# A two-layer fp32 trunk: activations and residual blocks turned through VectorE and device memory instead of TensorE

## The chip, the cores and the metric

One core of one Trainium2 chip runs the whole program in one launch. The metric is the device time of that launch in microseconds (us), median of several runs. Everything is computed and stored in fp32.

## What is computed

A sequence of 256 tokens with 2048 channels goes through two layers. Layer one is a Mamba-2 mixer, layer two a differential attention; a squared-ReLU MLP with 8192 hidden channels follows each of the two. Cut to what matters here:

```
h = h + mamba2_mixer(rms_norm(h, ssm_norm_w), ...)        # ends in y @ w_out, (256, 4096) @ (4096, 2048)
h = h + sq_relu_mlp(rms_norm(h, mlp_norm_w[0]), w_up[0], w_down[0])
k, v = shared_kv(h, kv_norm_w, w_kv, k_norm_w)
h = h + diff_attention(rms_norm(h, attn_norm_w), k, v, w_q, ..., w_o)
h = h + sq_relu_mlp(rms_norm(h, mlp_norm_w[1]), w_up[1], w_down[1])

def sq_relu_mlp(h, w_up, w_down):                          # w_up (2048, 8192), w_down (8192, 2048)
    return jnp.square(jax.nn.relu(h @ w_up)) @ w_down
```

## The kernel before

**Pieces.** All weights pass through the core once, in 865 pieces of 128 x 1024 numbers (512 KB). SyncE loads a piece into one of four slots of `w_raw`. ScalarE rounds it to the matmul's reduced fp32 format (`hi`, L739), VectorE subtracts the rounded part from the original (`lo`, L1093), and TensorE multiplies three times: stationary hi by weight hi (L366), hi by lo (L367), lo by hi (L368). In the stages around the change a piece is two tiles of 128 input channels by 512 output columns, so it costs 2 tiles x 2 token halves x 3 = 12 matmuls of 512 columns (`piece`, L351 to L369). The slots form a ring of four: `hi` of piece j waits until TensorE has finished piece j - 4 (semaphore `w_used`), and a load waits for `lo_made` of the piece four before.

**Order of work.** Every engine walks through the same list of pieces. All its other steps are written at hand-chosen places of this list: "if j == 2" means after the engine's own step for piece j. An engine does its steps in order, so a step that waits holds up the later pieces' `hi` or `lo`.

**MLP.** A chunk is 64 pieces. Its first 32 make four blocks u = 0..3 of 512 hidden channels (8 pieces each, `up`), its last 32 add the chunk's share to the four output blocks d = 0..3 (`down`). Each MLP has four chunks. A finished block u is read by ScalarE (`relu`, L919) and VectorE (`square`, L1298) into the buffer `act`, which has tokens on the partitions. The next product needs it with channels on the partitions, as the stationary operand `st`. So TensorE turns it: `turn_up` (L567) is eight 128 x 128 transposes through the identity matrix (L374) into a PSUM bank pair `aux`, and ScalarE (`up_hi`, L923) and VectorE (`up_lo`, L1302) split it from there into hi and lo.

**Residual blocks.** `h` is kept with tokens on the partitions. When a block n of 512 columns has been updated (`add_resid`, L1258 to L1268), `turn_resid` (L511) turns it on TensorE in the same way, and ScalarE (L744) and VectorE (L1098) split it with the norm's weight, once for the next MLP, twice for the attention (one copy for keys and values, one for queries).

**Banks.** Products alternate between the two PSUM bank pairs `acc[0]` and `acc[1]`; `aux[0]` and `aux[1]` hold turned blocks and the attention's or the scan's intermediate results.

**GpSimd.** Its instructions of the mixer end before the first MLP; after that it makes two masks and, once for every norm, a reciprocal square root (L1487).

The places of the steps, in pieces after the piece that completes a block, are these: add or relu and square two or three steps later, turn on TensorE after the third piece, split at the sixth. One table sets an order of pieces by hand:

```
WO_ORDER = ([(n, k) for n in (0, 1) for k in range(0, 12, 2)] + [(n, k) for n in (0, 1) for k in (12, 14)]
            + [(n, k) for n in (2, 3) for k in range(0, KT, 2)])
```

It is the list of (output block, input channel tile) for 32 pieces. The tiles 12 to 15 of block 0 come only after tiles 0 to 11 of block 1, so that the last quarter of the stationary operand is needed twelve pieces after the start and not six. Before the change only the attention's output product uses it.

## Time and profile before

| what | value |
|---|---|
| median of 3 runs | 2549.56 us (2549.36 to 2550.37) |
| the profiled execution | 2549.55 us, of which the trace spans 2547.9 us |
| TensorE matmul busy | 2524.6 us, 99% of the span |
| VectorE busy | 1477.1 us, 58% |
| ScalarE busy | 1194.0 us, 47% |
| GpSimd busy | 210.2 us, 8% |
| mean granted TensorE clock | 0.999 |

The span is the time from the first to the last instruction of the trace. The rest of the execution, 1.65 us, lies around it. Matmul durations in the rows overlap, since a matmul is drained while the next one streams; the pace is the distance between two starts.

### The profile page before, as it was taken

How to read it: one execution, taken by the hardware profiler on the slowest of the kernel's cores; microseconds unless marked ns; L12 is line 12 of the kernel's file. 1: busy time of each engine (PE TensorE's matmuls, PEld its weight loads, DVE VectorE, ACT ScalarE, POOL GpSimd, SP SyncE). 2: the span in 40 equal slices, each digit the busy share in tenths (PEclk: the TensorE clock that was granted, in tenths of full speed). 3: DMA queues.
4: the chain of work that ended last, by engine and by line, in shares of the span. 5: the costliest groups of instructions: out<-in, count | busy, mean ns of one | idle time of the engine just before them, and what ended most of it. 6: DMA issues, size and time to landing. Idle time of an engine off the chain costs nothing.

```text
span 2547.9 us, 33913 instructions
## 1 busy us (share of the span) xinstructions
PE 2524.6 (99%) x12081; PEld 2117.9 (83%) x12081; DVE 1477.1 (58%) x1508; ACT 1194.0 (47%) x1460; POOL 210.2 (8%) x115
## 2 busy tenths in 40 slices
PE   8999999999999999999999999999999999999999
PEld 7888888888888888888888888888888888888887
DVE  5777777775555555555555655666555555555554
ACT  5455555554444344344344545555544444443443
POOL 2433233330000000000000000000000000000000
PEclk9999999999999999999999999999999999999999
DMA  7555555554566565666665565554565666666664
GB/s 220 171 181 181 176 178 171 175 180 167 182 198 182 193 191 184 193 187 190 191 187 182 178 203 167 164 176 162 174 194 188 189 189 190 190 184 195 190 187 167
DMA packets 266592, 468.14 MB, mean 184 GB/s; under 512 B 17198, under 2 KB 50320, under 8 KB 265472
## 3 DMA queue, kind: packets, MB, share of 16 engines
q1 hardware_dynamic: 264736, 457.87, 58.6%
q0 software_dynamic: 1472, 8.79, 1.0%
q8 instruction: 72, 1.18, 0.2%
q14 instruction: 24, 0.20, 0.0%
q10 hardware_dynamic: 288, 0.11, 0.0%
HBM read 464.54 MB, written 2.16 MB: 183 GB/s over the span
## 4 chain that ended last, share of the span: by engine, by line
PE 88%; DVE 4%; issue 2%; POOL 2%; DMA 2%; ACT 2%; DVEq 0%; SPq 0%; ACTq 0%; POOLq 0%
PE acc L366 25%; PE acc L368 25%; PE acc L367 25%; PE aux L366 2%; PE aux L374 2%; PE aux L367 2%; PE aux L368 2%; DVE w_lo L1093 2%; DMA work<-decay_rows 1%; POOL work L1543 1%; POOL work L1541 1%; DVE work L1180 1%; ACT w_hi L739 1%; PE aux L435 1%; PE aux L434 1%
## 5 line engine op out<-in xcount | busy, mean ns | idle before, releaser
L1093 DVE TENSOR_TENSOR w_lo<-w_raw,w_hi 128x1024 fp32r<-128x1024 f32 x865 | 1121.4, 1301 | 821.4 <-ACT w_hi L739 819.9
L739 ACT ACTIVATE w_hi<-w_raw 128x1024 fp32r<-128x1024 f32 x865 | 913.3, 1060 | 1007.5 <-PE acc L368 904.6
L366 PE MATMUL acc<-w_hi,stationary 128*128 128x512 f32 x3200 | 1256.5, 393 | 1.9 <-DVE w_lo L1093 0.7
L368 PE MATMUL acc<-w_hi,stationary 128*128 128x512 f32 x3200 | 1246.4, 389 | 0.0
L367 PE MATMUL acc<-w_lo,stationary 128*128 128x512 f32 x3200 | 1245.7, 389 | 0.0
L368 PEld LDWEIGHTS acc<-w_hi,stationary 128*128 128x128 f32 x3200 | 600.6, 188 | 125.8
L366 PEld LDWEIGHTS acc<-w_hi,stationary 128*128 128x128 f32 x3200 | 601.0, 188 | 124.5 <-issue 1.1
L367 PEld LDWEIGHTS acc<-w_lo,stationary 128*128 128x128 f32 x3200 | 601.2, 188 | 121.2
L1487 POOL TENSOR_TENSOR small<-small 128x2 f32<-128x2 f32 (+2 forms) x22 | 38.3, 1744 | 1207.2 <-DVE small L1103 1207.2
L366 PE MATMUL aux<-w_hi,stationary 128*128 128x256 f32 (+1 forms) x384 | 123.8, 322 | 3.4 <-DVE w_lo L1093 3.4
L368 PE MATMUL aux<-w_hi,stationary 128*128 128x256 f32 (+1 forms) x384 | 122.2, 318 | 0.0
L367 PE MATMUL aux<-w_lo,stationary 128*128 128x256 f32 (+1 forms) x384 | 122.2, 318 | 0.0
L1302 DVE TENSOR_TENSOR stationary<-aux,stationary 128x1024 fp32r<-128x1024 f32 x32 | 39.2, 1224 | 74.5 <-ACT stationary L923 74.5
L366 PEld LDWEIGHTS aux<-w_hi,stationary 128*128 128x128 f32 x384 | 73.1, 190 | 10.9 <-DVE w_lo L1093 6.0
L374 PE MATMUL aux<-ident,work 128*128 128x128 f32 x576 | 75.7, 273 | 2.9 <-ACT work L824 2.9
L374 PEld LDWEIGHTS aux<-ident,work 128*128 128x128 f32 x576 | 66.7, 141 | 14.3 <-ACT work L824 5.9
L368 PEld LDWEIGHTS aux<-w_hi,stationary 128*128 128x128 f32 x384 | 73.0, 190 | 5.0
L367 PEld LDWEIGHTS aux<-w_lo,stationary 128*128 128x128 f32 x384 | 73.1, 190 | 4.9
L923 ACT ACTIVATE stationary<-aux 128x1024 fp32r<-128x1024 f32 x32 | 32.9, 1027 | 80.9 <-PE aux L374 80.9
L1098 DVE SCALAR_TENSOR_TENSOR stationary<-aux,params,stationary 128x256 fp32r<-128x256 f32 (+1 forms) x104 | 42.7, 474 | 44.3 <-ACT stationary L744 44.3
L1298 DVE SCALAR_TENSOR_TENSOR work<-acc,work 128x1024 f32<-128x1024 f32 x32 | 39.2, 1224 | 47.1 <-ACT work L919 47.1
L1555 POOL TENSOR_TENSOR work<-work 128x1024 f32<-128x1024 f32 (+1 forms) x16 | 59.7, 3729 | 59.1 <-ACT work L795 37.0
(173 smaller groups left out, 929.4 us busy)
## 6 DMA issues: line engine op xcount, KB each, us to landing
w_raw<-in_w_up SPq DMA_DIRECT2D x256, 512.0 KB
w_raw<-in_w_down SPq DMA_DIRECT2D x256, 512.0 KB
w_raw<-in_ssm_w_in SPq DMA_DIRECT2D x129, 512.0 KB
w_raw<-in_ssm_w_out SPq DMA_DIRECT2D x64, 512.0 KB
w_raw<-in_w_kv SPq DMA_DIRECT2D x64, 512.0 KB
w_raw<-in_ssm_w_in SPq DMA_DIRECT2D x64, 256.0 KB
w_raw<-in_w_q SPq DMA_DIRECT2D x32, 512.0 KB
w_raw<-in_w_o SPq DMA_DIRECT2D x32, 512.0 KB
```

The costliest lines, as they stand in the source:

```text
L366: pe.matmul(o, xh, hi[:, k], start=start, stop=False)
L367: pe.matmul(o, xh, lo[:, k], start=False, stop=False)
L368: mm = pe.matmul(o, xl, hi[:, k], start=False, stop=stop)
L374: tr = pe.transpose(dst(i, t), src(i, t), ident[:, :])
L739: a.activation(whi[:, s, :], raw[:, s, :], ACT.Copy).then_inc(sem("hi_made"), 1)
L923: a.activation(st[:, RB + 4 * u:RB + 4 * u + 4, 0, :], whole(aux[u % 2]), ACT.Copy).then_inc(sem("turned_hi"), 1)
L1093: v.tensor_tensor(wlo[:, s, :], raw[:, s, :], whi[:, s, :].bitcast(F32), ALU.subtract).then_inc(sem("lo_made"), 1)
L1098: ins = v.scalar_tensor_tensor(one_tile(st, kt + i, 1), turned_tile(bank, i), param(w + i), one_tile(st, kt + i, 0).bitcast(F32), ALU.mult ...
L1298: v.scalar_tensor_tensor(act, acc[u % 2][:, :, :], 0.0, act, ALU.max, ALU.mult).then_inc(sem("up_read"), 1)
L1302: v.tensor_tensor(st[:, RB + 4 * u:RB + 4 * u + 4, 1, :], whole(aux[u % 2]), st[:, RB + 4 * u:RB + 4 * u + 4, 0, :].bitcast(F32), ALU.subt ...
L1487: gp.tensor_tensor(out, in_, nhalf[:, 0:out.shape[1]], ALU.pow).then_inc(sem(signal), 1)
L1555: gp.tensor_tensor(m, m, c.unsqueeze(1).to_broadcast([P, HG, c.shape[1]]), ALU.mult).then_inc(sem("m_made"), 1)
```

## The change

The eight transposes of a block on TensorE go. In their place:

1. `turn` on VectorE: one instruction transposes each 32 x 32 square of the 128 x 1024 block, from `act` or `h` into the buffer `squares_t`.
2. `spread(n)` on GpSimd's queue: one DMA writes `squares_t` to a 512 KB scratch tensor in device memory; after it has landed, four DMAs, each for 32 partitions, read the squares back into `channels` in the places that they have in a full transpose. GpSimd does this 44 times. Both buffers lie in the arena `work`, in the place of the attention's `kT` and `qT`.
3. `resid_hi`, `resid_lo`, `up_hi`, `up_lo` read `channels` instead of `aux`.
4. The MLPs use all four bank pairs, block u or d in `banks[u]`, and their down products and first up products follow `WO_ORDER`. So does the first key and value product of the attention. SyncE loads the pieces in the same order.
5. The places of the steps are now in three tables, each row (block, piece that completes it, piece after which it is read and turned, piece after which it is split).

The diff, cut:

```
+UPS = ((0, 7, 10, 16), (1, 15, 18, 24), (2, 23, 26, 32), (3, 31, 34, 40))
+UPS_FIRST = ((0, 13, 15, 22), (1, 15, 17, 27), (2, 23, 26, 32), (3, 31, 34, 40))
+DOWNS = ((0, 45, 47, 54), (1, 47, 49, 59), (2, 55, 58, None))
+PLAIN = [(n, k) for n in range(4) for k in range(0, KT, 2)]
...
+        squares_t, channels = kT.rearrange("p s t -> p (s t)"), qT.rearrange("p s t -> p (s t)")
+        spread_dram = nc.dram_tensor("spread", [TT, 4, 32, 4, P], F32).ap()
+        banks = acc + aux
...
         def _(pe):
-            def turn_resid(n, added, turned):
-
-                pe.wait_ge(sem("resid_added"), added)
-                transposes(to_channels(aux[n % 2]), lambda i, t: h[:, t, n * NB + i * P:n * NB + (i + 1) * P]).then_inc(sem("turned"), 1)
...
+                def up(c, fresh):
+                    for i, (u, kt) in enumerate(WO_ORDER if fresh else PLAIN):
+                        if kt == 0:
+                            pe.wait_ge(sem("resid_added"), R + 4 * c + u - 3 if c else R - 1 if u == 0 else R)
+                        if fresh and u == 0 and kt % 4 == 0:
+                            pe.wait_ge(sem("turned_lo"), T - 3 + kt // 4)
+                        piece(Pos(base, c, PER_CHUNK), i, banks[u], NB, RA + kt, kt == 0, kt == KT - 2)
+
+                def down(c):
+                    for i, (d, kt) in enumerate(WO_ORDER):
+                        if kt == 0:
+                            pe.wait_ge(sem("up_read"), c * 4 + (U + d + 1))
+                        if d == 0 and kt % 4 == 0:
+                            pe.wait_ge(sem("turned_lo"), c * 4 + (T + 1 + kt // 4))
+                        piece(Pos(base, c, PER_CHUNK), 32 + i, banks[d], NB, RB + kt, kt == 0, kt == KT - 2)
...
         def _(act_e):
             def resid_hi(n, turned, targets):
-                a.wait_ge(sem("turned"), turned)
+                a.wait_ge(sem("spread"), turned * 64)
...
                 def up_hi(c, u):
+                    a.wait_ge(sem("spread"), c * 256 + (T + u + 1) * 64)
+                    a.activation(st[:, RB + 4 * u:RB + 4 * u + 4, 0, :].rearrange("p k (b i) -> p k b i", i=32),
+                                 channel_tiles, ACT.Copy).then_inc(sem("turned_hi"), 1)
...
         def _(v):
+            def turn(src, n):
+
+                wait(v, sem("spread_out"), (n - 1) * 16)
+                v.transpose(squares_t.rearrange("p (t q k i) -> p t k q i", q=4, k=4, t=TT),
+                            src.rearrange("p t (k q i) -> p t k q i", k=4, q=4)).then_inc(sem("turned"), 1)
...
                 def square(c, u):
 
                     v.wait_ge(sem("relu_made"), c * 4 + (U + u + 1))
-                    v.scalar_tensor_tensor(act, acc[u % 2][:, :, :], 0.0, act, ALU.max, ALU.mult).then_inc(sem("up_read"), 1)
+                    v.scalar_tensor_tensor(act, banks[u][:, :, :], 0.0, act, ALU.max, ALU.mult).then_inc(sem("up_read"), 1)
+                    v.wait_ge(sem("up_read"), c * 4 + (U + u + 1))
+                    turn(act, c * 4 + (T + u + 1))
...
+                        for d, last, at_add, at_lo in DOWNS:
+                            if j == at_add:
+                                add_resid(d, Pos(base, c, PER_CHUNK), last, True, banks[d])
+                                if carry:
+                                    turn_resid(d, R + 13 + d, T_carry + d + 1)
+                            if j == at_lo and carry:
+                                resid_lo(d, T_carry + d + 1, after)
...
         def _(gp):
+            def spread(n):
+
+                gp.wait_ge(sem("turned"), n)
+                wait(gp, sem("spread"), (n - 1) * 64)
+                gp.dma_start(spread_dram.rearrange("t b c q f -> (b c) t (q f)"),
+                             squares_t.rearrange("p (t f) -> p t f", t=TT)).then_inc(sem("spread_out"), 16)
+                gp.wait_ge(sem("spread_out"), n * 16)
+                wait(gp, sem("turned_lo"), n - 1)
+                for q in range(4):
+                    gp.dma_start(channels[32 * q:32 * q + 32, :].rearrange("c (b f) -> c b f", f=P),
+                                 spread_dram[:, :, :, q, :].rearrange("t b c f -> c (t b) f")).then_inc(sem("spread"), 16)
```

`carry` is true in the last chunk of the first MLP, whose updated residual blocks go to the attention. The attention's output product uses the rows of `DOWNS` less 32. A last block (n = 3) is always added and turned after the third piece of the next stage and split after its ninth.

How instructions move, at three places. On TensorE in the first MLP, where block u = 1 of the first chunk is turned, the order before is (matmul rows L366 to L368 are the three products, L374 the transposes, `lo_made`, `turned_lo`, `up_read`, `resid_added` semaphores):

```order
L368 MATMUL acc<-w_hi,stationary 128x512
L374 MATMUL aux<-ident,work 128x128 [waits turned_lo,up_read]
L374 MATMUL aux<-ident,work 128x128 x7
L366 MATMUL acc<-w_hi,stationary 128x512 [waits lo_made]
L367 MATMUL acc<-w_lo,stationary 128x512
```

Now, in the same stretch of the program, block u = 2 begins in a bank pair `aux` and nothing stands between the pieces:

```order
L396 MATMUL acc<-w_hi,stationary 128x512
L394 MATMUL aux<-w_hi,stationary 128x512 [waits lo_made,resid_added]
L395 MATMUL aux<-w_lo,stationary 128x512
L396 MATMUL aux<-w_hi,stationary 128x512
L394 MATMUL aux<-w_hi,stationary 128x512
```

Over the whole program, TensorE's list has 61 groups of L374 before and 17 of the same line (now L402) after: 44 groups have gone. On VectorE, after block u = 0 of the first chunk (`w_lo` is the piece's `lo`, `work` the activation buffer), before:

```order
L1298 SCALAR_TENSOR_TENSOR work<-acc,work 128x1024 [waits relu_made]
L1091 REGISTER_ALU
L1093 TENSOR_TENSOR w_lo<-w_raw,w_hi 128x1024 [waits hi_made]
L1091 REGISTER_ALU
L1093 TENSOR_TENSOR w_lo<-w_raw,w_hi 128x1024 [waits hi_made]
L1091 REGISTER_ALU
L1093 TENSOR_TENSOR w_lo<-w_raw,w_hi 128x1024 [waits hi_made]
L1301 REGISTER_ALU
L1302 TENSOR_TENSOR stationary<-aux,stationary 128x4x256 [waits turned_hi]
```

and now, with the transpose of squares after each square, two blocks read two pieces apart, and the split moved away:

```order
L1284 SCALAR_TENSOR_TENSOR work<-acc,work 128x1024 [waits relu_made]
L1244 STREAM_TRANSPOSE work<-work 128x2x4x4x32 [waits spread_out,up_read]
L1063 TENSOR_TENSOR w_lo<-w_raw,w_hi 128x1024 [waits hi_made] x2
L1284 SCALAR_TENSOR_TENSOR work<-acc,work 128x1024 [waits relu_made]
L1244 STREAM_TRANSPOSE work<-work 128x2x4x4x32 [waits spread_out,up_read]
L1063 TENSOR_TENSOR w_lo<-w_raw,w_hi 128x1024 [waits hi_made] x5
L1291 TENSOR_TENSOR stationary<-work,stationary 128x4x256 [waits turned_hi]
```

On GpSimd, right behind the masks, where nothing stood before but the norm's root, 44 groups like these two now follow, split by the attention's roots:

```order
L1557 DMA spread<-work 128x2x512 [waits spread,turned]
L1562 DMA work<-spread 32x8x128 [waits turned_lo,spread_out]
L1562 DMA work<-spread 32x8x128 x3
L1557 DMA spread<-work 128x2x512 [waits spread,turned]
L1562 DMA work<-spread 32x8x128 [waits turned_lo,spread_out]
```

The reads wait twice: for their own write to land, and until VectorE has split the block before (`turned_lo`), since there is one `channels` buffer.

## Rows read from the trace of the kernel before

**Rows 1.** The page: busy time, share of the span and instructions of each engine

```profile
PE 2524.6 (99%) x12081; PEld 2117.9 (83%) x12081; DVE 1477.1 (58%) x1508; ACT 1194.0 (47%) x1460; POOL 210.2 (8%) x115
```

**Rows 2.** Windows: chunk-long stretches of both MLPs, each engine's busy us, clock, DMA, GB/s

```profile
core 0: us, PE busy (x) PEld busy (x) DVE busy (x) ACT busy (x) POOL busy (x), PEclk, DMA share, GB/s
760.00:938.00 178.00, 178.00 (x803) 147.76 (x802) 93.05 (x81) 75.22 (x72) 0.00 (x0) 1.00 0.63 190
2014.00:2192.00 178.00, 178.00 (x803) 147.73 (x803) 92.72 (x80) 75.56 (x73) 0.00 (x0) 1.00 0.63 189
```

**Rows 3.** Waits of TensorE: who it waited for, us in total, times, longest

```profile
PE aux L366 <- DVE w_lo L1093: 3.4, 6, 0.6
PE acc L366 <- DVE stationary L1098: 0.6, 1, 0.6
```

**Rows 4.** Timeline of TensorE: two turns one chunk apart, then one turn with its neighbours

```profile
760.87 1.04 PE L374 MATMUL aux<-ident,work 128*128 128x128 f32 x8
...
938.55 1.04 PE L374 MATMUL aux<-ident,work 128*128 128x128 f32 x8
...
1316.11 0.39 PE L367 MATMUL acc<-w_lo,stationary 128*128 128x512 f32 x1
1316.33 0.40 PE L368 MATMUL acc<-w_hi,stationary 128*128 128x512 f32 x1
1316.57 1.04 PE L374 MATMUL aux<-ident,work 128*128 128x128 f32 x8
1317.36 0.48 PE L366 MATMUL acc<-w_hi,stationary 128*128 128x512 f32 x1
1317.68 0.40 PE L367 MATMUL acc<-w_lo,stationary 128*128 128x512 f32 x1
```

**Rows 5.** Timelines after a block ends: TensorE's next matmul, ScalarE, VectorE

```profile
1308.40 0.39 PE L366 MATMUL acc<-w_hi,stationary 128*128 128x512 f32 x1
...
1308.60 1.03 ACT L919 ACTIVATE work<-acc 128x1024 f32<-128x1024 f32 x1 [1.60 <-PE acc L368]
...
1309.66 1.22 DVE L1298 SCALAR_TENSOR_TENSOR work<-acc,work 128x1024 f32<-128x1024 f32 x1 [1.40 <-ACT work L919]
1310.80 1.21 DVE L1093 TENSOR_TENSOR w_lo<-w_raw,w_hi 128x1024 fp32r<-128x1024 f32 x1
```

**Rows 6.** Groups of instructions by form: VectorE's and ScalarE's passes

```profile
L1302 DVE TENSOR_TENSOR stationary<-aux,stationary 128x1024 fp32r<-128x1024 f32 x32 | 39.2, 1224 | 74.5 <-ACT stationary L923 74.5
L923 ACT ACTIVATE stationary<-aux 128x1024 fp32r<-128x1024 f32 x32 | 32.9, 1027 | 80.9 <-PE aux L374 80.9
L889 ACT ACTIVATE work<-resid 128x512 f32<-128x512 f32 x24 | 14.9, 623 | 1.7 <-DVE resid L1267 0.6
```

**Rows 7.** Timelines of ScalarE and VectorE: a residual block split twice; an add

```profile
1453.58 3.03 ACT L744 ACTIVATE stationary<-aux,params 128x256 fp32r<-128x256 f32 x8 [2.48 <-PE aux L374]
...
1456.64 3.23 DVE L1098 SCALAR_TENSOR_TENSOR stationary<-aux,params,stationary 128x256 fp32r<-128x256 f32 x8 [4.28 <-ACT stationary L744]
...
2522.14 1.41 DVE L1267 SCALAR_TENSOR_TENSOR resid<-acc,small,resid 128x512 f32<-128x512 f32 x2 [0.34 <-PE acc L368]
```

**Rows 8.** DMA issues: KB each, median us from issue to landing

```profile
work<-decay_rows POOLq DMA_DIRECT2D x8, 1024.0 KB, 5.0
resid<-in_x SPq DMA_DIRECT2D x4, 512.0 KB, 7.5
out<-resid SPq DMA_DIRECT2D x3, 512.0 KB, 5.9
out<-resid SPq DMA_DIRECT2D x2, 256.0 KB, 2.2
decay_rows<-work POOLq DMA_DIRECT2D x1, 64.0 KB, 2.0
```

**Rows 9.** The page, DMA queues: packets, MB, share of 16 engines; a GpSimd issue

```profile
q1 hardware_dynamic: 264736, 457.87, 58.6%
...
L1528 POOL DMA_DIRECT2D work<-decay_rows x8 | 4.9, 612 | 215.3 <-PE aux L435 213.7 <-DMA decay_rows<-work 1.7
```

**Rows 10.** Waits of ScalarE for weight loads, the two longest totals

```profile
ACT w_hi L739 <- DMA w_raw<-in_ssm_w_in: 14.1, 10, 2.0
ACT w_hi L739 <- DMA w_raw<-in_w_down: 9.4, 4, 3.0
```

**Rows 11.** Timeline of VectorE in the mixer, a `lo` beside a GpSimd pass

```profile
122.37 3.01 DVE L1093 TENSOR_TENSOR w_lo<-w_raw,w_hi 128x1024 fp32r<-128x1024 f32 x1 [2.35 <-ACT w_hi L739]
```

More of the change, by code:

```diff
@@ L957, in _ @@
+                chunk(0, True, False)
+                with a.Fori(1, 3) as c:
+                    chunk(c, False, False)
+                chunk(3, False, after is not None)
             mlp(UP0, R_MLP0, T_MLP0, 0, T_MLP0_END, to_mlp0, to_att)
@@ L1347, in _ @@
+                chunk(0, True, False)
+                with v.Fori(1, 3) as c:
+                    chunk(c, False, False)
+                chunk(3, False, after is not None)
             mlp(UP0, R_MLP0, T_MLP0, 0, T_MLP0_END, to_mlp0, to_att,
```

287 lines of the change are left out of this document (118 added, 169 removed).

## The prediction

> **What bounds the kernel now.** I read the page first: TensorE's matmuls are busy for 99% of the span, VectorE for 58%, ScalarE for 47% [rows 1]. Such a share could still hide pauses inside a stage, so the windows come next: a stretch of 178 us in either MLP shows matmuls for all of it, at full clock, with VectorE busy half of the time and the DMA engines 63% [rows 2]. Then the waits: what TensorE waited for is a few us in all, a total of 3.4 us being the largest one on the path of the pieces [rows 3]. So every us of TensorE's own work that goes shortens the run, and every us by which another engine makes it wait lengthens it. VectorE and ScalarE need only keep ahead.
>
> **What goes: 44 turns.** The order lists show 44 groups of eight transposes fewer on TensorE: 12 residual blocks and 2 x 16 activation blocks. The price of one is read from starts, since durations overlap. The last matmul before a turn starts at 1316.33, the second after it at 1317.68 [rows 4]: 1.35 us where two pitches would stand. The pitch comes from two turns one chunk apart: 938.55 - 760.87 = 177.68 us hold 64 x 12 matmuls and four turns [rows 4]. With c = 1.35 - 2p, 768p + 4c = 177.68 gives p = 0.2267 us and c = 0.897 us. The rows are rounded to 10 ns, so I take 0.895: 44 x 0.895 = **39.4 us** off the bound engine. A piece is 12p = 2.72 us.
>
> **What comes: nothing on TensorE, but three chains that must stay hidden.** Let t be the moment at which TensorE starts the piece after the one that completes a block.
>
> *First chain, the ring.* TensorE may run on while VectorE reads and turns the block. Before, relu starts 0.20 after t and square follows; the next `lo` starts 2.40 after t and ends at 3.61 [rows 5]. Now the transpose of squares stands between, of length T. It waits for the square's own semaphore, say 0.1, so the next `lo` ends at about 3.7 + T. In most places three pieces are ready by then (8.16 us), so T may be 4.4. Tight are the blocks u = 0 and 1 of each MLP's first chunk, read two pieces after they end: two pieces ready, 5.44 us, T up to 1.7. The same distance holds for d = 0 and 1 where residual blocks are turned (end of MLP 0, attention's output product), but there the add costs 1.41 [rows 7] instead of relu and square: 0.2 + 1.41 + 0.1 + T + 1.21 leaves T up to 2.5. No transpose of squares is in this trace. The nearest rows are VectorE's passes over the same 128 x 1024 fp32: 1.22 [rows 6]; the dearest such pass, slowed beside GpSimd's work, is 3.01 [rows 11]. I take 1.22, since one operand streams through just as in the cheap ones and GpSimd now only issues DMAs. Cost 0. At 3.01 the four tight reads lose 1.3 each and the four tight adds 0.5 each: 7.2 us. That is the upper bound; below zero it can't be, as no wait of TensorE stood there.
>
> The Trainium skill (VectorE: DVE Perf Modes, The three transpose paths) gives 311 ns for one 128 x 128 bf16 transpose of squares; if a block costs eight of these, an estimate by this page of the Trainium skill, T is 2.5 us and the run loses 4 x 0.8 = 3.2 us more than in my sum. No row here has the operation. The same page's rules for kernel authors say to turn 128 x 128 on TensorE when PSUM is a fit destination, which speaks against this change; the trace shows why it need not hold here, as TensorE is the one engine without idle time [rows 1].
>
> *Second chain, the way through memory.* Square and transpose end at about 2.5 + T = 3.8 after t. Then GpSimd issues the write (0.61 an issue [rows 9]), waits until it lands, issues four reads, waits for the last. Landing times from issue are 2.0 us for 64 KB out, 5.9 for 512 KB out, 2.2 for 256 KB, 5.0 for 1 MB in beside the weight stream, 7.5 for 512 KB in at the very start [rows 8]. I take 5.0 for the write and for the last read, because this row is from the same queue under the same load: 3.8 + 5.0 + 3 x 0.61 + 5.0 + 0.2 = **15.8 us** after t; bounds 2.0 and 2.0 give 9.8, and 5.9 and 7.5 give 19.2. When is it needed? The split stands nine pieces after the block's last piece. TensorE wants the next `lo` at 9 x 2.72 = 24.5; before it come the hi split 1.03 and lo split 1.22 [rows 6] and that `lo`, 1.21, with hand-overs 3.7. So the landing may be as late as 20.8. ScalarE gets there at about 14.9 and waits a us, which costs nothing. Even the upper bound fits. The operand itself is needed later still, at the thirteenth down piece. Cost 0 for 32 activation blocks.
>
> *Third chain, residual blocks for the attention.* These are split twice, 3.03 on ScalarE and 3.23 on VectorE [rows 7], so the limit falls to 24.5 - 7.7 = 16.8 after t, against 2.9 + 5.0 + 1.8 + 5.0 + 0.2 = 14.9. In addition the reads of one block wait until the block before is split. Block 1 is the tight one: ScalarE squares block 2 first (two passes with their sums, 1.6 us [rows 6, 7]), is free 3.2 after the end of piece 55, and 7.7 later the next `lo` is done, at 10.9, where TensorE wants it at 4 x 2.72 = 10.9. Block 2 lands about 1.5 after ScalarE could take it and ends 0.4 before its limit. With the landing bounds instead, blocks 0 and 2 lose 1 to 2 us each and block 1 as much again: 0 to 5. I take **1.0** for the whole stage change. For MLP 1 the blocks are split once, which halves the splits, and it fits.
>
> *DMA.* A turn adds 0.5 MB out and 0.5 MB back, 46 MB in all. At the price of the weight queue, 58.6% of the span for 457.87 MB [rows 9], that is 5.9% more, so the share goes from 0.60 to 0.66. One turn's traffic can delay one weight load by about 3.3 us. ScalarE has waited for loads before, 3.0 us at most, and TensorE noticed none of it [rows 10], for three pieces are ready ahead. Cost 0, covered by the ring.
>
> *Bank pairs and the new orders* remove waits that already cost nothing [rows 3]. VectorE gets 44 x 1.22 = 54 us more, of the 1070 us in which it is idle. GpSimd's roots stand in line behind the spreads, and the attention's first use is now at its piece 16, so they are early. The tail after the last piece is the same.
>
> **Sum.** 2549.55 (the profiled execution; the median of the three runs is 2549.56, so no correction) - 39.4 + 1.0 = **2511.2 us**, 1.5% faster.
>
> **Rivals.**
> 1. *The issue of small row pieces makes GpSimd's queue slow, and the run is slower.* A turn has 256 rows of 2 KB out and 1024 of 512 B back, in five issues; the issue of 0.61 us [rows 9] was for fewer and longer rows. Each issue lies in the second chain: with 2.4 us each, four times the row, the landing moves from 15.8 to 15.8 + 5 x 1.8 = 24.8, TensorE waits 4.0 for each of 44 blocks, 2511 + 176 = 2687. It decides from 20.8 on; gain and loss meet at 20.8 + 0.9 = 21.7. For it: the shape is in no row. Against: one issue for 64 KB and one for 1 MB land with the difference of their bytes only [rows 8], and the upper bounds above leave 1.6 us of room. The Trainium skill (DMA: Bandwidth & Descriptors, Anatomy of one DMA) puts the generation of descriptors down as small, with many for little more, and a DMA at 2.0 us plus its bytes over 436 GB/s, which would make the landing 3.8 + 3.2 + 1.8 + 2.3 + 0.2 = 11.3; it also warns of a long delay when device memory is written. Chance 0.07.
> 2. *The transpose of squares takes several passes.* With T = 4 x 1.22 = 4.9: the 28 ordinary reads lose 0.5 each, the four tight ones 3.2, the four tight adds 2.4: 36 us, 2547, no change. For it: an fp32 element is four bytes and the pattern has five levels. Against: every fp32 pass in the trace goes at one pace. Chance 0.05.
> 3. *Weight loads come late.* If the mixed traffic holds up loads so that TensorE loses 0.5 us in each turn, 2511 + 22 = 2533. Against it is the reserve above. Chance 0.05.
>
> Remains 0.83 for the forecast. Its own range is from 2510 (no stall) to 2511 + 7 + 4 = 2522 (both upper bounds). **Range** 2509.5 to 2523: it leaves out all three rivals, 0.17, and little else. About 0.2% (5 us) is what a measurement of this kernel can tell from no change. Faster by more: forecast, rival 3 and a mild form of 2, 0.90; the same 0.03; slower 0.07.
>
> **What would show it.** In the profile after: matmul pitch 0.2267 and 174.1 us per chunk instead of 177.7; 352 transposes on TensorE fewer; a transpose row of about 1.2 us x44; ScalarE waiting about 1 us for the reads before each `up_hi`, and the last read landing near 16 us after t; a wait of TensorE for `lo` of 0 to 2 us at the start of the attention and nowhere else. Wrong would be: TensorE waiting for `lo` in every chunk (second chain or loads), or in the first chunks only (T over 1.7).

## The result: 25.1 us faster, 13 us less than forecast

| | before | after |
|---|---|---|
| median | 2549.55 us (2549.36 to 2550.37, 4 runs) | 2524.43 us (2523.01 to 2525.01, 4 runs) |
| ratio, 95% interval | | 0.990 (0.9883 to 0.9917) |
| the profiled execution, its span | 2549.55, 2547.9 | 2525.01, 2523.4 |
| mean granted TensorE clock | 0.999 | 0.998 |

The direction was right, the size was not: 2511.2 was forecast, and the measured median lies 1.4 us above the upper end of the range, 2523.0. In what follows t is, as in the prediction, the moment at which TensorE starts the piece after the one that completes a block.

The page after, busy time [rows 1], DMA queues [rows 9] and the two new kinds of issue on GpSimd's queue (median us from issue to landing in the last column of the last two rows):

```profile
PE 2490.2 (99%) x11729; PEld 2083.6 (83%) x11729; DVE 1523.5 (60%) x1552; ACT 1192.5 (47%) x1460; POOL 344.4 (14%) x335
...
q1 hardware_dynamic: 264736, 457.87, 59.0%
q0 software_dynamic: 16256, 54.94, 8.2%
...
L1557 POOL DMA_DIRECT2D spread<-work x44 | 31.9, 725 | 1226.0 <-DVE work L1244 1070.2
L1562 POOL DMA_DIRECT2D work<-spread x176 | 102.2, 587 | 168.5 <-DMA spread<-work 147.7
...
spread<-work POOLq DMA_DIRECT2D x44, 512.0 KB, 3.8
work<-spread POOLq DMA_DIRECT2D x176, 128.0 KB, 6.0
```

TensorE has the 352 transposes fewer. GpSimd's issues cost 0.725 us for the write and 0.587 for a read. The 6.0 us are the median of all 176 reads; the last of the four, for which ScalarE waits, lands a median of 7.4 us after its own issue in this trace. The same stretch of MLP 0 as in [rows 2]:

```profile
core 0: us, PE busy (x) PEld busy (x) DVE busy (x) ACT busy (x) POOL busy (x), PEclk, DMA share, GB/s
760.00:938.00 178.00, 178.00 (x787) 147.34 (x786) 100.61 (x88) 77.48 (x75) 15.22 (x25) 1.00 0.74 219
1390.00:1460.00 70.00, 60.19 (x255) 48.33 (x253) 41.08 (x60) 38.20 (x63) 10.71 (x16) 0.96 0.67 206
```

In the chunk TensorE is busy all the time at full clock, as hoped. The second row is the passage from MLP 0 to the attention, and there 70 us hold only 60.2 of matmuls, at a granted clock of 0.96. The waits name it. TensorE's rows for `lo` (L1063, which answers to L1093 in [rows 3]), then ScalarE's for DMAs, of which the weight loads answer to [rows 10]:

```profile
PE aux L394 <- DVE w_lo L1063: 8.8, 9, 2.2
PE acc L394 <- DVE w_lo L1063: 5.8, 2, 5.0
```

```profile
ACT stationary L895 <- DMA work<-spread: 84.1, 30, 6.4
ACT w_hi L712 <- DMA w_raw<-in_w_down: 19.8, 7, 6.4
ACT stationary L870 <- DMA work<-spread: 18.6, 8, 7.0
ACT w_hi L712 <- DMA w_raw<-in_w_up: 17.1, 11, 3.8
ACT w_hi L712 <- DMA w_raw<-in_w_kv: 7.1, 3, 4.2
```

**Where the time went.** Between 1398 and 1461 us TensorE stops four times. From start to start (a pitch is 0.227) the distances are 2.48 at 1398.32, 2.59 at 1414.30, 1.42 at 1432.03 and 5.44 at 1455.12; less the pitches 11.0 us, and 0.7 more in the first step after each. Behind the second and the fourth the matmuls start 0.427 apart for 7 and 10 steps, which is the lower of the clock's two levels, 1.2 GHz, and costs 17 x 0.2 = 3.4. Together 15.1 us. The forecast without any stall is 2549.55 - 39.4 = 2510.15, and the profiled execution took 14.9 more. So the budget closes: **39.4 us were gained as computed, and some 15 were given back in one place.** The fourth stop:

```profile
1455.12 0.39 PE L396 MATMUL acc<-w_hi,stationary 128*128 128x512 f32 x1
1460.56 0.79 PE L394 MATMUL acc<-w_hi,stationary 128*128 128x512 f32 x1 [5.05 <-DVE w_lo L1063]
1461.15 0.63 PE L395 MATMUL acc<-w_lo,stationary 128*128 128x512 f32 x1
```

How this comes about is read from three timelines of the same stretch (in brackets: idle time before the row and what ended it). ScalarE:

```profile
1392.06 1.06 ACT L712 ACTIVATE w_hi<-w_raw 128x1024 fp32r<-128x1024 f32 x1 [4.48 <-DMA w_raw<-in_w_down]
1393.03 3.29 ACT L870 ACTIVATE stationary<-work,params 128x256 fp32r<-128x256 f32 x8
...
1406.50 1.06 ACT L712 ACTIVATE w_hi<-w_raw 128x1024 fp32r<-128x1024 f32 x1 [6.36 <-DMA w_raw<-in_w_down]
...
1409.10 3.31 ACT L870 ACTIVATE stationary<-work,params 128x256 fp32r<-128x256 f32 x8 [1.54 <-DMA work<-spread]
...
1425.66 3.31 ACT L870 ACTIVATE stationary<-work,params 128x256 fp32r<-128x256 f32 x8 [3.00 <-DMA work<-spread]
...
1452.78 3.31 ACT L870 ACTIVATE stationary<-work,params 128x256 fp32r<-128x256 f32 x8 [6.99 <-DMA work<-spread]
```

VectorE, from the split of block 0 (L1257) to the add of block 3 (L1238) and the split of block 3:

```profile
1396.35 3.26 DVE L1257 SCALAR_TENSOR_TENSOR stationary<-work,params,stationary 128x256 fp32r<-128x256 f32 x8 [1.97 <-ACT stationary L870]
1399.52 4.62 DVE L1063 TENSOR_TENSOR w_lo<-w_raw,w_hi 128x1024 fp32r<-128x1024 f32 x4
...
1429.00 3.26 DVE L1257 SCALAR_TENSOR_TENSOR stationary<-work,params,stationary 128x256 fp32r<-128x256 f32 x8 [5.08 <-ACT stationary L870]
1432.18 2.35 DVE L1063 TENSOR_TENSOR w_lo<-w_raw,w_hi 128x1024 fp32r<-128x1024 f32 x2
1434.45 1.40 DVE L1238 SCALAR_TENSOR_TENSOR resid<-aux,small,resid 128x512 f32<-128x512 f32 x2
...
1456.12 3.25 DVE L1257 SCALAR_TENSOR_TENSOR stationary<-work,params,stationary 128x256 fp32r<-128x256 f32 x8 [9.07 <-ACT stationary L870]
```

GpSimd:

```profile
1377.25 0.72 POOL L1557 DMA_DIRECT2D spread<-work  x1 [30.77 <-DVE work L1244]
1381.03 2.32 POOL L1562 DMA_DIRECT2D work<-spread  x4 [3.05 <-DMA spread<-work]
1390.17 0.72 POOL L1557 DMA_DIRECT2D spread<-work  x1 [6.82 <-DMA work<-spread]
1400.16 2.32 POOL L1562 DMA_DIRECT2D work<-spread  x4 [9.27 <-DVE stationary L1257]
1409.62 0.72 POOL L1557 DMA_DIRECT2D spread<-work  x1 [7.13 <-DMA work<-spread]
```

The reader is to see a loop. Block 0's reads land by 1390.2, 6.8 us after GpSimd has issued the last of them; but `hi` of the next piece stands before the split, and a weight load ends its wait only at 1392.06. The double split stops VectorE until 1399.6, and then four `lo` stand in a row (x4). A load waits for the `lo` of the piece four before it, so these loads go out in a bunch; the first `hi` that depends on them gets its data at 1406.50, after 6.36 us of idling. Meanwhile block 1's write has waited for block 0's reads (1390.17), its reads for block 0's split (1400.16), and the add of block 3, whose pieces were done at 1429.5, comes at 1434.45, because VectorE has block 2's split (until 1432.3) and two late `lo` to do first. Nobody is busy for the whole time: each waits for another.

The prediction had a limit for this stage: the data of a block that is split twice must be there 16.8 us after its t. By the same working, block 1, which is split after twelve pieces and not nine, has 8.2 us more, and every pause that TensorE has made since t gives a block as much more. Set against this limit, the timelines account for each of the four stops (all in us; t from TensorE's timeline, the start of the split from ScalarE's):

| block | t | split starts, after t | limit, with pauses and slow steps since t | too late by | TensorE's stop, less a pitch |
|---|---|---|---|---|---|
| 0 | 1374.07 | 19.0 | 16.8 | 2.2 | 2.25 |
| 1 | 1379.51 | 29.6 | 16.8 + 8.2 + 2.3 = 27.3 | 2.3 | 2.36 |
| 2 | 1403.65 | 22.0 | 16.8 + 4.1 = 20.9 | 1.1 | 1.19 |
| 3 | 1429.54 | 23.2 | 16.8 + 1.3 = 18.1 | 5.1 | 5.21 |

Block 0's reads were there in time (16.1 at the latest); its split is late by the weight load before it and by that piece's `hi`. The other three wait for their reads. So the limit was right and the time at which the data are there was wrong.

### The profile page after: what moved, and what is told of

Its sections match the earlier page's. It is cut to its first block, busy times and chain, and to the rows that moved or that the text cites. A ratio compares the mean times of both kernels' runs of the same rounds, so it can differ in the third digit from the quotient of the medians.

```text
span 2523.4 us, 32793 instructions
## 1 busy us (share of the span) xinstructions
PE 2490.2 (99%) x11729; PEld 2083.6 (83%) x11729; DVE 1523.5 (60%) x1552; ACT 1192.5 (47%) x1460; POOL 344.4 (14%) x335
## 4 chain that ended last, share of the span: by engine, by line
PE 73%; issue 9%; DMA 8%; DVE 4%; POOL 3%; ACT 2%; DVEq 0%; ACTq 0%; POOLq 0%; SPq 0%
PE acc L394 14%; PE acc L396 14%; PE acc L395 14%; PE aux L394 9%; PE aux L395 9%; PE aux L396 9%; DMA work<-spread 4%; DVE w_lo L1063 2%; DMA spread<-work 2%; DMA work<-decay_rows 1%; PE aux L402 1%; POOL work L1562 1%; POOL work L1528 1%; POOL work L1526 1%; DVE work L1150 1%
## 5 line engine op out<-in xcount | busy, mean ns | idle before, releaser
L1063 DVE TENSOR_TENSOR w_lo<-w_raw,w_hi 128x1024 fp32r<-128x1024 f32 x865 | 1109.5, 1294 | 728.0 <-ACT w_hi L712 725.3
L394 PE MATMUL acc<-w_hi,stationary 128*128 128x512 f32 x2176 | 855.5, 393 | 7.1 <-DVE w_lo L1063 5.8
L396 PE MATMUL acc<-w_hi,stationary 128*128 128x512 f32 x2176 | 848.2, 390 | 0.0
L395 PE MATMUL acc<-w_lo,stationary 128*128 128x512 f32 x2176 | 848.0, 390 | 0.0
L394 PE MATMUL aux<-w_hi,stationary 128*128 128x512 f32 (+1 forms) x1408 | 523.0, 371 | 8.8 <-DVE w_lo L1063 8.8
L396 PE MATMUL aux<-w_hi,stationary 128*128 128x512 f32 (+1 forms) x1408 | 521.3, 370 | 0.0
L395 PE MATMUL aux<-w_lo,stationary 128*128 128x512 f32 (+1 forms) x1408 | 521.3, 370 | 0.0
L394 PEld LDWEIGHTS acc<-w_hi,stationary 128*128 128x128 f32 x2176 | 409.1, 188 | 92.1 <-DVE w_lo L1063 6.0
L396 PEld LDWEIGHTS acc<-w_hi,stationary 128*128 128x128 f32 x2176 | 408.9, 188 | 85.9
L395 PEld LDWEIGHTS acc<-w_lo,stationary 128*128 128x128 f32 x2176 | 409.3, 188 | 83.1
L394 PEld LDWEIGHTS aux<-w_hi,stationary 128*128 128x128 f32 x1408 | 265.7, 189 | 57.6 <-DVE w_lo L1063 12.6
L396 PEld LDWEIGHTS aux<-w_hi,stationary 128*128 128x128 f32 x1408 | 265.6, 189 | 45.0
L395 PEld LDWEIGHTS aux<-w_lo,stationary 128*128 128x128 f32 x1408 | 265.6, 189 | 44.9
L1562 POOL DMA_DIRECT2D work<-spread x176 | 102.2, 587 | 168.5 <-DMA spread<-work 147.7
L895 ACT ACTIVATE stationary<-work 128x1024 fp32r<-128x1024 f32 x32 | 33.9, 1060 | 84.1 <-DMA work<-spread 84.1
L1150 DVE SCALAR_TENSOR_TENSOR work<-aux,params,work 128x255 f32<-128x255 f32 (+1 forms) x144 | 58.1, 468 | 0.0
L402 PE MATMUL aux<-ident,work 128*128 128x128 f32 x320 | 42.5, 274 | 2.6 <-ACT work L797 2.6
```

Of the source, the lines that this page charges most:

```text
L394: pe.matmul(o, xh, hi[:, k], start=start, stop=False)
L395: pe.matmul(o, xh, lo[:, k], start=False, stop=False)
L396: mm = pe.matmul(o, xl, hi[:, k], start=False, stop=stop)
L402: tr = pe.transpose(dst(i, t), src(i, t), ident[:, :])
L895: a.activation(st[:, RB + 4 * u:RB + 4 * u + 4, 0, :].rearrange("p k (b i) -> p k b i", i=32), channel_tiles, ACT.Copy).then_inc(sem("turn ...
L1063: v.tensor_tensor(wlo[:, s, :], raw[:, s, :], whi[:, s, :].bitcast(F32), ALU.subtract).then_inc(sem("lo_made"), 1)
```

## The experiments

"Before" was run beside each batch: medians 2550.23 (e1 to e4), 2550.18 (e5 to e8), 2550.38 (e9 to e11), 2549.11 (e12), against 2549.55 beside the change. So a difference between batches is uncertain by about 1 us. Each run has 4 executions where no number is given.

**e1: the attention's four residual blocks turned on TensorE again**, the other 40 left as changed.

```
+DOWNS_PE = ((0, 45, 47, 51), (1, 47, 49, 54), (2, 55, 58, 61))
...
+                            for n, at in ((0, 48), (1, 50), (2, 58)):
+                                if 32 + i == at:
...
+                                    turn_resid(n, R + 13 + n, acc[n % 2])
...
+                    if first and i == 2:
+                        pe.wait_ge(sem("turned_lo"), T_MLP0_END + 2)
+                        turn_resid(3, R_WO, acc[1])
```

> The four residual blocks that go to the attention are turned on TensorE again, all 40 others stay on the new way. Theory A (the missing 14 us sit in the chain of these four blocks: write, reads, two splits, each waiting for the one before): the four pauses of TensorE at the change from the first MLP to the attention, 2.4, 2.4, 1.3 and 5.6 us with about 3.8 us of half clock behind two of them, all go, and 4 x 0.89 = 3.6 us come back: 2524.4 - 15.3 + 3.6 = 2512.7 us. Theory B (the transfers slow the weight loads everywhere): TensorE still waits for lo there or in other chunks, 2518 us or more.

Measured 2515.03 us (2513.95 to 2515.94), ratio 0.9863 (0.9847 to 0.9880): 9.4 us faster than the change, although it pays for four turns, 3.6. Only 40 turns saved would be 2549.56 - 35.8 = 2513.8. The stops at the passage are gone:

```profile
PE aux L396 <- DVE w_lo L1082: 3.5, 6, 0.6
```

This is the fastest kernel of the study that does all the work, and it shows that the loss sits in these four blocks and not in the 32 activation blocks.

**e2: two buffers** (`channels`, scratch tensor and semaphore alternate between two blocks), so that reads need not wait for the block before to be split.

```
-                wait(gp, sem("spread"), (n - 1) * 64)
+                wait(gp, sem(f"spread{n % 2}"), (n - 1) // 2 * 64)
...
-                wait(gp, sem("turned_lo"), n - 1)
+                wait(gp, sem("turned_lo"), n - 2)
```

> Two channels buffers (the attention's kq is the second), two scratch tensors, two semaphores for the reads. The write of a block no longer waits for the reads of the block before, nor the reads for its split. Theory A1 (the queue between the blocks is the main cost): blocks 1 and 3 land about 8 us earlier, the pauses shrink to those of the long double splits, 2515 to 2518 us. Theory B (late weight loads): the same traffic comes in a shorter time, so nothing is gained, 2523 to 2527 us.

Measured 2519.82 (2517.57 to 2523.47), ratio 0.9878 (0.9862 to 0.9895): 4.6 us of the 15, with executions 6 us apart. The line of blocks behind one another is a part of the cause. In the profiled execution, the slowest of the four, a stop of 5.8 stays at the attention's ninth piece, and new ones of 1 to 2 us appear in chunks.

**e3: one split instead of two** for these blocks; the queries' copy of the operand is left out and the queries are computed from the keys' copy.

```
-            to_mlp0, to_att, to_mlp1 = [(RA, N_MLP0)], [(RA, N_KV), (RC, N_ATT)], [(RA, N_MLP1)]
+            to_mlp0, to_att, to_mlp1 = [(RA, N_MLP0)], [(RA, N_KV)], [(RA, N_MLP1)]
```

> The residual blocks for the attention are split once, not twice (the copy with the queries' norm weights is left out, and the query product reads the keys' copy): 3.3 us on ScalarE and 3.3 us on VectorE become about 1.9 each. Theory A2 (the double split is what fills the ring): most of the pauses go, about 2513 us. Theory A1 (the waits between blocks): the reads of the next block start 3 us earlier, the pauses shrink by about half, 2517 us. Theory B: nothing, 2524 us.

Measured 2515.47 (2514.83 to 2516.51), ratio 0.9865 (0.9848 to 0.9881): 9.0 us back. With each block holding ScalarE and VectorE for half as long, the loop mostly opens.

**e4: the traffic alone.** The kernel before, with its turns on TensorE, and beside them the change's write and four reads a block; nothing on the path waits for them.

```
+            def spread(n):
+                gp.wait_ge(sem("turned"), n)
+                wait(gp, sem("spread"), (n - 1) * 64)
...
+                    gp.dma_start(channels[32 * q:32 * q + 32, :].rearrange("c (b f) -> c b f", f=P),
+                                 spread_dram[:, :, :, q, :].rearrange("t b c f -> c (t b) f")).then_inc(sem("spread"), 16)
```

> The kernel before, with TensorE's turns, plus the same 44 writes and 176 reads issued by GpSimd after each turn; nobody uses their data, and only the attention's first kT waits for them. Theory A: 2549.6 us, since a late weight load stays inside the ring. Theory B: TensorE waits for lo, 2555 us or more; ScalarE's waits for weight loads grow in either case.

Measured 2550.10 (2549.35 to 2551.18, 10 runs) beside 2550.23, ratio 1.000 (0.999 to 1.001). The loads are late more often than in [rows 10], and it costs nothing:

```profile
PE aux L368 <- DVE w_lo L1096: 3.4, 6, 0.6
```

```profile
ACT w_hi L741 <- DMA w_raw<-in_w_down: 14.8, 6, 5.3
ACT w_hi L741 <- DMA w_raw<-in_w_kv: 11.8, 4, 3.9
```

A wait of 5.3 us for a load goes unnoticed while three pieces are ready ahead. So the zero that the prediction put on DMA holds for the traffic by itself.

**e5 and e6: the two splits apart**, the queries' copy made two or three pieces after the other (e5), and the same with e2's two buffers (e6).

```
+                                if at_hi and j == at_hi + 2:
+                                    resid_hi(d, T_carry + d + 1, to_query)
```

> The keys' and the queries' copies of an attention residual block are split at two places, the second one two or three pieces later; one channels buffer as in the change, so the reads of the next block wait for the second split. Theory A2 (one long stop of 3.3 us on ScalarE and 3.3 us on VectorE uses up the ring): as with one split, 2515 to 2517 us. Theory A1 (reads wait for the split): the reads of blocks 1 to 3 start even later, 2520 us or more.

> Two split places and two channels buffers together. If the pauses come from the long stop plus the queue between blocks, both are gone and what is left is TensorE's bound of 2549.6 - 39.4 plus 1 or 2 us: 2511 to 2513 us. If late weight loads do it (theory B), the two places of late loads remain, 2516 us or more.

Measured 2520.31 (2519.35 to 2521.51), ratio 0.9882 (0.9866 to 0.9899), and 2517.74 (2516.83 to 2519.61), ratio 0.9872 (0.9856 to 0.9889). Shorter stops give 4.1 us back, both edits together 6.7. With a single buffer the next block's reads now wait for the later of the two splits, so e5 takes with one hand what it gives with the other. Neither reaches e3, so the work of the second copy seems to count, and not only its length in one go. e6 ends in the range that I had named for late weight loads (2516 or more); its largest stop, 3.9 us from start to start at 1451.9, is again the last block's.

**e7 and e8: one and three small DMAs** of 32 bytes, each waited for, between the write and the reads of every block.

```
                 gp.wait_ge(sem("spread_out"), n * 16)
+                for i in range(1):
+                    gp.dma_start(pause, nhalf[0:1, :]).then_inc(sem("paused"), 16)
+                    gp.wait_ge(sem("paused"), ((n - 1) * 1 + i + 1) * 16)
```

> The change with one more small GpSimd DMA of 32 bytes, and the wait for it, between write and reads of every block: all reads land about 2 us later, with no traffic to speak of. In the MLP chunks ScalarE waits for the reads 2.6 us on average from 14.9 on, so they land at 17.5 and 2 more stay within the limit of 20.8; only the four attention blocks lose, up to 2 us each: 2526 to 2532 us. If the chunks had no room left, 40 blocks lose about 2 us: 2600 us.

> The same with three small DMAs, about 6 us later. The reads land at about 23.5, which is 2.7 over the limit: 32 activation blocks lose 2.7 each, the residual blocks 3 to 6: 2524 + 86 + 40 = 2650 us, with TensorE waiting for lo once in each block. If the limit of 20.8 is wrong and the ring gives more room, 2540 us.

Measured 2652.05 (2638.72 to 2659.38), ratio 1.0410 (1.0391 to 1.0428), and 2807.83 (2805.19 to 2810.42), ratio 1.1014 (1.0996 to 1.1033). I had put the hop too low, at 2 us. The small DMA's time from issue to landing in e7 is

```profile
DMA to landing us min/median/max: 1.6/4.1/6.5
```

and with its hand-overs the hop adds 4.9 us between the issue of the write and that of the first read (medians 9.0 in e7 and 4.1 in the change). That is more than the 20.8 - 17.5 = 3.3 us between the measured landing and the prediction's limit, so TensorE waits in every chunk. A block that follows one in time loses about what it is over the limit: the first one of MLP 0's second chunk lands 22.0 us after t and costs 1.1. The three behind it land at 26.4, 29.0 and 26.9, each pushed by the one before. The mean cost is 127.6 / 44 = 2.9 us a block.

**e11: a shorter delay without a DMA**, five memsets of a spare buffer between the landing of the write and the reads.

```
+                for i in range(5):
+                    gp.memset(no_later[:, :], 0.0).then_inc(sem("paused"), 1)
+                    gp.wait_ge(sem("paused"), (n - 1) * 5 + i + 1)
```

> The changed kernel with five short GpSimd memsets of a spare 128 x 128 buffer, each waiting for the one before, between the landing of the write and the reads: no DMA more, 5 x (0.21 + about 0.1) = 1.5 us later landing of every block's reads, 19.0 and not 17.5 us after t. It measures how much room the chunks have, with nothing added to the DMA engines. If room ends where the prediction put it (20.8 us), only the end of MLP 0 loses, some 4 x 1.5 = 6 us: 2530. If the room is the 1 to 3 us that one more small DMA (4.1 us, +2.9 us a block) suggests, most chunks still lose nothing at 1.5 us: 2530 to 2540. Over 2560 the room is nil and the changed kernel stands at the cliff in every chunk.

Measured 2546.07 (2541.37 to 2554.38, 10 runs), ratio 0.9987 (0.9977 to 0.9997): 21.6 us lost, over both forecasts of mine though below 2560. The memsets are 45.2 us in 220, 1.03 us a block, with hand-overs 1.3:

```profile
L1561 POOL MEMSET no_later<- 128x128 f32 x220 | 45.2, 206 | 172.2 <-DMA spread<-work 162.1
```

Inside MLP 0 TensorE's starts stand 3.7 us apart at 818.0 and 2.3 at 1019.3, and ScalarE's waits for w_down and w_up go from 19.8 and 17.1 to 79.4 and 57.0 us. The second of these stops, with t in the first row and the split, which waited for the reads, in the second:

```profile
995.02 0.39 PE L394 MATMUL acc<-w_hi,stationary 128*128 128x512 f32 x1
1018.05 1.06 ACT L895 ACTIVATE stationary<-work 128x1024 fp32r<-128x1024 f32 x1 [7.51 <-DMA work<-spread]
1019.31 0.39 PE L396 MATMUL acc<-w_hi,stationary 128*128 128x512 f32 x1
1021.56 0.50 PE L394 MATMUL acc<-w_hi,stationary 128*128 128x512 f32 x1 [1.87 <-DVE w_lo L1063]
```

The data are there 23.0 us after t, 2.2 over the limit of 20.8, and the stop is 2.25 less a pitch, 2.0. The same reading for the 30 activation blocks with this limit (u = 1 of a first chunk is split twelve pieces after its end and has 29.0):

| | landing after t: median, lowest to highest | over 20.8 |
|---|---|---|
| the change | 17.4, 15.0 to 21.2 | 1, at a cost of 0.3 us |
| e11 | 20.4, 16.7 to 26.2 | 9, and TensorE loses time behind these nine and behind no other |

So the limit holds to 0.2 us. What the sum lacked is the spread of the landings, and that a delay grows on its way: 1.3 us of it move the median by 3.0. A late block makes the `lo` behind it late, these make loads late, and the next block is read and written out later. At the passage to the attention the profiled execution stops for 10.2 us, against 11.0 in the change; what it loses more, it loses in the chunks and, 2.9 us, in front of MLP 1. The times also begin to scatter, from 2541 to 2554.

**e9: a quarter of the bytes.** The same five issues, the same waits, the same splits, but 128 KB out and 4 x 32 KB back; the rest of the turned buffer keeps old numbers.

```
-                gp.dma_start(spread_dram.rearrange("t b c q f -> (b c) t (q f)"),
-                             squares_t.rearrange("p (t f) -> p t f", t=TT)).then_inc(sem("spread_out"), 16)
+                gp.dma_start(spread_dram.rearrange("t b c q f -> (b c) t (q f)")[:, :, 0:P],
+                             squares_t.rearrange("p (t f) -> p t f", t=TT)[:, :, 0:P]).then_inc(sem("spread_out"), 16)
```

> The changed kernel, with the same five issues a block, but the write takes only the first 128 of each 512 numbers of a partition's half (256 rows of 512 B) and the reads 1024 rows of 128 B: 0.25 MB a block through device memory and not 1 MB. The rest of the turned buffer keeps old numbers, so the activations that the products read are not the reference's. Theory A (at the end of MLP 0 it is the time of the way itself, the latency and the queue of the blocks behind one another, that holds the splits up): landing times fall only by the bytes, to about 4 us for the write and 4.5 for the reads, 2 to 3 us a block less; the pauses of TensorE there go from 15 to 7 or so, total 2516 to 2518. Theory B (the traffic delays the weight loads, and these delay lo): ScalarE's waits for w_down, 19.8 us in 7 with 6.4 the longest, fall to the 9.4 in 4 of the kernel before, and the pauses go to 3 or less: 2511 to 2513. Theory C (neither, the two long splits of each block do it alone): no change, 2522 to 2525.

Measured 2512.10 (2511.29 to 2512.46), ratio 0.9849 (0.9832 to 0.9865). That is 0.9 us from the forecast, with every dependency of the change in place. ScalarE's waits:

```profile
ACT w_hi L712 <- DMA w_raw<-in_w_up: 6.5, 5, 2.1
ACT stationary L870 <- DMA work<-spread: 5.1, 3, 2.9
ACT w_hi L712 <- DMA w_raw<-in_w_down: 3.2, 2, 1.8
ACT stationary L895 <- DMA work<-spread: 2.4, 2, 1.8
```

With a quarter of the bytes, the single buffers, the queue behind them and the long splits cost one stop of 1.3 us, where block 3's data are there 18.0 after t against the limit of 16.8 (theory C falls). With e4 it makes a cross: traffic without the dependencies costs 0, dependencies with little traffic 2, both together 14 to 15. Theory B's number came true, but the edit shortens the way and frees the loads at once, so it can't say which.

**e12: e9 plus the missing bytes** in DMAs that nobody on the path waits for, issued right behind the small reads.

```
+                gp.dma_start(rest_out.rearrange("p (r f) -> p r f", f=P), no_later[:, :].unsqueeze(1).to_broadcast([P, 6, P])).then_inc(sem("rest"), 16)
+                for q in range(4):
+                    gp.dma_start(spare[32 * q:32 * q + 32, :].rearrange("c (b f) -> c b f", f=P)[:, :, 0:96],
```

> The kernel of e9_quarter, which waits for small DMAs only, with the missing bytes moved by DMAs that nobody on the path waits for: right behind the four small reads GpSimd issues one write of 384 KB from a constant buffer to a spare tensor in device memory and four reads of 96 KB each from a weight tensor into a spare buffer. It has 1 MB a block again, five issues (about 3 us) more on GpSimd's queue, and each block's spare DMAs wait for those of the block before. As in e9_quarter three quarters of the turned buffer keep old numbers. Theory B' (bytes that delay the weight loads cause the pauses by themselves): ScalarE's waits for w_down and w_up go back to 15 to 30 us each and the pauses at the end of MLP 0 come back: 2519 to 2526. Theory A' (a block's own bytes make its own way long; the weight loads are late mainly because the splits are, and loads are then issued in bunches): the small reads still land early, the splits start in time, and TensorE has little to wait for: 2511 to 2515.

Measured 2515.88 (2515.09 to 2517.17), ratio 0.9869 (0.9852 to 0.9885): between the two theories, nearer to A'. ScalarE's waits for loads come back to about what theory B' asked for, 15 us each, and those for the blocks do not:

```profile
ACT w_hi L714 <- DMA w_raw<-in_w_down: 14.9, 6, 4.4
ACT w_hi L714 <- DMA w_raw<-in_w_up: 13.6, 9, 5.0
ACT w_hi L714 <- DMA w_raw<-in_w_kv: 11.1, 6, 2.8
ACT stationary L872 <- DMA work<-spread: 5.6, 3, 2.9
```

So, by difference, late loads are worth 2515.9 - 2512.1 = 3.8 us, and the blocks' own longer way 2524.4 - 2515.9 = 8.5. Taken by the ratios to "before", 0.9849, 0.9869 and 0.990, the shares are 5.1 and 8. Neither split is sharp: e12 also carries five issues more on GpSimd's queue, and its spare bytes move behind the block's reads and not with them.

**e10: without device memory.** Sixteen DMAs a block go from buffer to buffer, half the bytes and one hop.

```
+                for b in range(4):
+                    for q in range(4):
+                        gp.dma_start(channels[32 * q:32 * q + 32, :].rearrange("c (t b f) -> c t b f", t=TT, f=P)[:, :, b, :],
+                                     squares_t[32 * b:32 * b + 32, :].rearrange("c (t q f) -> c t q f", q=4, t=TT)[:, :, q, :]).then_inc(sem("spread"), 16)
...
-                wait(v, sem("spread_out"), (n - 1) * 16)
+                wait(v, sem("spread"), (n - 1) * 256)
```

> The changed kernel without device memory: sixteen GpSimd DMAs a block move each row of squares from the buffer on 32 partitions straight to its 32 partitions in the other buffer, 256 B... 512 B a row, 0.5 MB a block in one hop and not 1 MB in two; the DVE transpose of the next block waits for the last of them. Sixteen issues at the 0.59 us that a read's issue takes now are 9.4 us, and a landing of about 4 us stands behind the last: 3.9 + 9.4 + 4 = 17.3 us after t, the same as the 17.5 now. Theory A (latency and queue): the queue holds each block as long as before, so the pauses at the end of MLP 0 stay, 2520 to 2526; if an issue costs more than 0.59 us on this shape, each chunk waits too and the time goes over 2530. Theory B (traffic and late loads): half the traffic brings half the pauses back, 2516 to 2519.

Measured 2558.20 (2557.17 to 2560.19, 8 runs), ratio 1.0033 (1.0022 to 1.0044), slower than before. Not through a dearer issue, which is 0.535 us: it is a wait that I mentioned and didn't cost. VectorE may turn the next block only when the last of sixteen DMAs has landed, and where two blocks end two pieces apart it stands still with the `lo` behind it:

```profile
773.22 1.23 DVE L1284 SCALAR_TENSOR_TENSOR work<-acc,work 128x1024 f32<-128x1024 f32 x1 [0.69 <-ACT work L891]
780.30 1.25 DVE L1244 STREAM_TRANSPOSE work<-work 128x1024 f32<-128x1024 f32 x1 [5.86 <-DMA work<-work]
```

There TensorE's starts stand 5.5 us apart at 777.2, and it goes on 0.427 apart, at the lower clock, for eleven matmuls. The test of half the traffic is spoilt by this; whether a second `squares_t` would mend it wasn't tried.

## Why the prediction was right and where it failed

- **44 turns by 0.895 us** held, and a chunk takes the forecast 174.1 us. e9 and e1, which have almost no stall, stand 1.9 and 1.2 us above what it gives (2510.2 and 2513.8). In e9 about 1 us of that lies ahead of everything that was changed: the same step of the mixer that stands at 591.19 in the kernel before stands at 592.22 there.
- **First chain, the ring.** T was taken as 1.22 from VectorE's other passes. It is 1.246, and the two-piece reads of the first chunks showed no stop:

```profile
L1244 DVE STREAM_TRANSPOSE work<-work x32: 1245/1246/1248, 767.3 to 2434.7; 128x1024 f32<-128x1024 f32 x32
```

  (min/median/max in ns.) The estimate by the Trainium skill (VectorE: DVE Perf Modes, The three transpose paths), 2.5 us for a block, is twice this; by this case's runs, the rule of the same page of the Trainium skill (Rules for kernel authors) to prefer TensorE for a 128 x 128 turn was wrong for the 40 blocks with time and, by e1, right for the four without, though for a reason of the schedule and not of the operation. Rival 2 is out.
- **Second chain.** 15.8 us after t were forecast, 19.2 was the upper bound. The write landed in 3.8 us and not 5.0, the last read in 7.4 and not 5.0. ScalarE, expected to wait about 1 us, waits 84.1 / 32 = 2.6 a block on top of the 14.9, so the data come near 17.5, 1.7 later than forecast. The **limit of 20.8 was right**: e11's stops begin where it puts them. That a single landing time stands for all blocks was not right. They spread from 15.0 to 21.2, so the upper bound of 19.2 was too low, and the latest, in MLP 1, cost the only 0.3 us that the chunks lost. With the next block pushed by a late one, the room is less than 20.8 less the median says: e11 used it up with 1.3 us.
- **Third chain.** This is the step that failed: taken at 1.0 with 5 as the upper bound, it cost about 15. Its limit of 16.8 held at each of the four stops; the landing of 14.9 that was set against it did not. The data were there, or the split could start, 19.0, 29.6, 22.0 and 23.2 us after t. Three things were missing. (1) The bounds moved the landing, block by block, with the loads in time and no carry-over; in the trace block 0's delay goes on to blocks 1, 2 and 3. I had written that the reads wait for the block before. The **write** waits for its reads too (block 1's squares are turned at 1382.4, its write is issued at 1390.17), and I didn't count that, nor that the add of block 3 would come 4.9 us after its pieces, behind a late split and two late `lo`. (2) The DMA term was costed apart, "covered by the ring", and the ring's three pieces were at the same time given to the double split of 6.6 us. One reserve was spent twice: block 0's stop of 2.25 us is a weight load's wait of 4.5 and the double split together, while e4 has waits of up to 5.3 for loads and loses nothing. (3) After the second and the fourth stop TensorE went on at half its clock, 3.4 us that stood in no term.
- **DMA.** The bytes added 5.9% in the estimate; in the pages the weight queue's share went from 58.6 to 59.0 and the second queue's from 1.0 to 8.2, 7.6 together, while the MLP's share rose from 0.63 to 0.74. Alone that costs nothing (e4). With splits that wait for it, e9 and e12 put some 4 to 5 us of the loss on late loads and 8 on the slower way of the blocks.
- **Rival 1** (slow issues) is out: 0.587 and 0.725 us, as in [rows 9], and the time didn't rise. But its mechanism, a later landing in each of 44 blocks, is real, as e7 and e11 show. It sets in at the 20.8 that I gave it, but block by block and not for the median. **Rival 3** (late loads cost in each turn) was right that loads come late and wrong on the place: not 0.5 us in 44 turns, but at one passage.
- The sign that was named, "a wait of TensorE for `lo` of 0 to 2 us at the start of the attention and nowhere else", was nearly right on the place, the passage from MLP 0 to the attention, and wrong on the size.

What stays open: the 15 us aren't a sum of independent parts (e2 4.6, e3 9.0, e5 4.1, e9 12.3, each alone), so no edit has "its" share; and how much of the carry-over between blocks is due to the write's wait alone wasn't tried.

## What to carry to other kernels

Where an engine has a reserve of ready work, list everything that draws on it in the same stretch (a long step, a late load, a late block) and set the sum of the delays against it once; costing each against the full reserve gives zero for all of them. Work moved off the bound engine is best moved where its result isn't wanted soon: here 40 of 44 blocks, and leaving four on the bound engine for 3.6 us beat moving all by 9.4. Where many blocks pass one limit, set the latest against it and not the median: here 17.4 and 21.2 against 20.8. A small delay put into the path shows how much room is left in truth: 1.3 us a block cost 21.6.

## What the hardware showed that I had not expected

- A DMA of 32 bytes, issued by GpSimd while weights stream at about 200 GB/s, takes 4.1 us from issue to landing (1.6 to 6.5), as long as one of 512 KB (3.8). By the Trainium skill (DMA: Bandwidth & Descriptors, Anatomy of one DMA), a DMA costs some 2.0 us plus its bytes; the shortest here, 1.6, lies a little under that, the median beside the weights is twice it.
- Four reads of 128 KB in rows of 512 B land later (6.0, the last of them 7.4) than the single write of 512 KB in rows of 2 KB (3.8); with rows of a quarter the median of all five falls from 5.7 to 3.9.
- The granted clock fell to its lower level right after the start distances of 2.59 and 5.44 us in the changed kernel, but not after those of 2.48 at 1398.32 and 1.42 at 1432.03.
- Five memsets of 0.2 us each on an engine that is busy for 14% of the span cost this kernel 21.6 us.
